# Softmax weights transposed on VectorE and through HBM instead of on TensorE, in a four-layer encoder

## What is computed

```python
logits = jnp.einsum('bqhmd,bkhmd->bmhqk', qb, k).astype(jnp.float32) + bias
probs = jax.nn.softmax(logits, axis=-1)
w = (probs[:, 0] - lam * probs[:, 1]).astype(v.dtype)
return jnp.einsum('bhqk,bkhe->bqhe', w, v)
...
logits = jnp.einsum('bshd,bmhd->bhsm', q, km).astype(jnp.float32)
probs = jax.nn.softmax(logits, axis=-1).astype(vm.dtype)
return jnp.einsum('bhsm,bmhd->bshd', probs, vm).reshape(b, s, XATTN_W)
```

## Time and profile before

| | |
|---|---|
| median of 3 runs | 1246.14 us (1246.03 to 1246.64) |
| span of the profiled execution | 1244.7 us |
| TensorE busy | 1235.2 us, 99%, 7370 instructions |
| VectorE busy | 1024.4 us, 82% |
| ScalarE busy | 730.3 us, 59% |
| DMA engines, mean busy share of the weight queue | 55.5%, 229.27 MB moved |

### The profile page before, as it was taken

How to read it: one execution, slowest core, us unless ns; L and a number is a source line. 1 busy time by engine, 2 the same in 40 slices (tenths; PEclk the granted TensorE clock), 3 DMA queues, 4 the chain that set the end, 5 groups by cost and what they waited for, 6 DMA issues and landing times.

```text
span 1244.7 us, 19689 instructions
## 1 busy us (share of the span) xinstructions
PE 1235.2 (99%) x7370; PEld 1082.9 (87%) x7370; DVE 1024.4 (82%) x1599; ACT 730.3 (59%) x1190; POOL 20.1 (2%) x29
## 2 busy tenths in 40 slices
PE   9999999999999999999999999999999999999997
PEld 7988888888999988888889888888888888888886
DVE  5876888889779888988887978988888776988887
ACT  6675765555766546555555546655554774755552
POOL 0001000000000100000000000000000001000000
PEclk9999999999999999999999999999999999999999
DMA  9834576554553345655655764656554533666651
GB/s 333 285 120 136 190 248 190 186 192 163 175 182 119 122 150 169 227 187 195 201 173 168 233 204 162 227 195 199 190 186 169 187 119 119 218 207 201 196 190 54
DMA packets 64539, 229.27 MB, mean 184 GB/s; under 512 B 7575, under 2 KB 9239, under 8 KB 63421
## 3 DMA queue, kind: packets, MB, share of 16 engines
q1 hardware_dynamic: 64444, 228.02, 55.5%
HBM read 226.93 MB, written 1.06 MB: 183 GB/s over the span
## 4 chain that ended last, share of the span: by engine, by line
PE 97%; DMA 1%; SPq 1%; DVE 0%; issue 0%; ACT 0%; DVEq 0%
PE pair L768 28%; PE acc L862 21%; PE pair L771 14%; PE pair L800 4%; PE pair L801 4%; PE pair L802 4%; PE acc L768 2%; PE acc L843 2%; PE acc L842 2%; PE acc L841 2%; PE pair L1022 2%; DMA raw<-in_stream 1%; PE pair L825 1%; PE pair L827 1%; PE pair L829 1%; PE acc L931 1%
## 5 line engine op out<-in xcount | busy, mean ns | idle before, releaser
L1278 DVE TENSOR_TENSOR w_lo<-raw,w_hi 128x1024 fp32r<-128x1024 f32 x400 | 482.6, 1221 | 105.3 <-ACT w_hi L1040 103.7
L1040 ACT ACTIVATE w_hi<-raw 128x1024 fp32r<-128x1024 f32 x400 | 420.5, 1058 | 213.2 <-PE pair L771 70.8
L768 PE MATMUL pair<-xT,w_hi 128*128 128x512 f32 x1520 | 477.8, 396 | 0.0
L771 PEld LDWEIGHTS pair<-xT,w_lo 128*128 128x128 f32 x1520 | 285.5, 188 | 67.2
L771 PE MATMUL pair<-xT,w_lo 128*128 128x256 f32 x1520 | 298.6, 278 | 0.0
L768 PEld LDWEIGHTS pair<-xT,w_hi 128*128 128x128 f32 x1520 | 233.8, 189 | 3.2 <-issue 0.3
L1087 ACT ACTIVATE hid<-pair 128x512 f32<-128x512 f32 x88 | 52.6, 597 | 124.9 <-PE pair L771 124.9
L1319 DVE TENSOR_TENSOR hid<-pair,hid 128x512 f32<-128x512 f32 x88 | 60.7, 690 | 47.9 <-ACT hid L1087 47.7
L800 PE MATMUL pair<-xT,w_hi 128*128 128x256 f32 x336 | 97.8, 291 | 0.0
L801 PE MATMUL pair<-xT,w_hi 128*128 128x256 f32 x336 | 95.0, 283 | 0.0
L802 PE MATMUL pair<-xT,w_lo 128*128 128x256 f32 x336 | 94.9, 283 | 0.0
(11 more groups left out here) (223 smaller groups left out, 1661.9 us busy)
## 6 DMA issues: line engine op xcount, KB each, us to landing
raw<-in_stream SPq DMA_DIRECT2D x400, 512.0 KB, 4.6
gains<-in_ln SPq DMA_DIRECT2D x8, 1024.0 KB, 8.4
bias<-bias_scratch SPq DMA_DIRECT2D x2, 1152.0 KB, 9.0
raw<-in_stream SPq DMA_DIRECT2D x8, 256.0 KB, 6.6
x_tok<-in_x_t SPq DMA_DIRECT2D x4, 256.0 KB, 6.2
y_tok<-in_mem_t SPq DMA_DIRECT2D x2, 512.0 KB, 7.1
x_tok<-in_x SPq DMA_DIRECT2D x1, 1024.0 KB, 6.5
out<-x_tok SPq DMA_DIRECT2D x4, 256.0 KB, 2.0
```

The lines of the kernel that those rows point to most:

```text
L768: pe.matmul(bank, w_hi[:, slot, kk * P:(kk + 1) * P], xT[:, kk].rearrange("p a s -> p (a s)"), start=(kk == 0), stop=(kk == KT - 1), skip_ ...
L771: last = pe.matmul(bank[:, 0:SEQ], w_lo[:, slot, kk * P:(kk + 1) * P], xT[:, kk, 0, :], start=False, stop=(kk == KT - 1), skip_group_check ...
L1040: nc.scalar.activation(w_hi[:, u % SPLIT, :], raw[:, u % RAW, :], ACT.Copy).then_inc(hi_ready, 1)
L1278: v.tensor_tensor(w_lo[:, u % SPLIT, :], raw[:, u % RAW, :], w_hi[:, u % SPLIT, :].bitcast(F32), ALU.subtract).then_inc(lo_ready, 1)
```

## The change

TensorE no longer transposes the softmax weights. VectorE transposes them in 32x32 blocks ("xswap", "swap"): each block is turned in itself and stays in its band of 32 partitions. Four DMAs from SyncE's queue (one for each band) store the result to a scratch tensor in HBM, in rows of 256 floats (cross-attention) or 128 floats (heads), and one DMA ("xfetch", "fetch") reads it back so that the blocks stand in their transposed places. The scratch of each matrix is its own. The cross-attention's fetch lands where "xpv" reads it, in blocks (strided), and the heads' one is copied to `probT` by ScalarE ("spread"). In layer 1 the product "xprob" moves from VectorE to ScalarE. SyncE now walks the list of items as well, with the loads of weights in their places (`next_unit`), and the store of a swap waits for VectorE, the fetch for the four stores. In layers 0 and 3, "pv" of heads 4 and 5, "ms", "tok" and "scale" of the last pairs come one or more halves later.

```diff
-            at = {0: [it("xlog", 0), it("xlog", 1)], 1: [it("xexp", 0)], 2: [it("xexp", 1), it("xprob", 0)],
-                  3: [it("xprob", 1)], 5: [it("log", 0), it("log", 1)],
-                  6: [it("exp", 0), it("xturn", 0)], 7: [it("exp", 1), it("xpv", 0)],
-                  8: [it("prob", 0), it("xturn", 1)], 9: [it("prob", 1), it("xpv", 1), it("log", 2), it("log", 3), it("turnw", 0)],
-                  10: [it("exp", 2)], 11: [it("turnw", 1), it("exp", 3), it("prob", 2)],
-                  12: [it("prob", 3)], 13: [it("turnw", 2), it("log", 4), it("log", 5), it("pv", 0), it("pv", 1)],
-                  14: [it("ms", 0), it("exp", 4)], 15: [it("turnw", 3), it("tok", 0), it("exp", 5), it("prob", 4)],
-                  16: [it("scale", 0), it("prob", 5)], 18: [it("turnw", 4), it("pv", 2), it("pv", 3), it("turnw", 5)],
-                  19: [it("pv", 4), it("pv", 5), it("ms", 1), it("tok", 1), it("ms", 2)], 20: [it("scale", 1), it("tok", 2)],
-                  21: [it("scale", 2)]}
+            at = {0: [it("xlog", 0), it("xlog", 1)], 1: [it("xexp", 0)], 2: [it("xexp", 1), it("xprob", 0), it("xswap", 0)],
+                  3: [it("xprob", 1), it("xswap", 1), it("xfetch", 0)], 4: [it("xfetch", 1)],
+                  5: [it("log", 0), it("log", 1)], 6: [it("exp", 0)], 7: [it("exp", 1), it("xpv", 0)],
+                  8: [it("prob", 0), it("swap", 0)],
+                  9: [it("prob", 1), it("swap", 1), it("xpv", 1), it("log", 2), it("log", 3), it("fetch", 0)],
+                  10: [it("exp", 2), it("fetch", 1)], 11: [it("exp", 3), it("prob", 2), it("swap", 2)],
+                  12: [it("prob", 3), it("swap", 3), it("fetch", 2)],
+                  13: [it("log", 4), it("log", 5), it("pv", 0), it("pv", 1), it("fetch", 3)],
+                  14: [it("ms", 0), it("exp", 4)], 15: [it("tok", 0), it("exp", 5), it("prob", 4), it("swap", 4)],
+                  16: [it("scale", 0), it("prob", 5), it("swap", 5), it("fetch", 4)], 17: [it("fetch", 5)],
+                  18: [it("pv", 2), it("pv", 3)], 19: [it("ms", 1), it("tok", 1)],
+                  20: [it("scale", 1), it("pv", 4), it("pv", 5)], 21: [it("ms", 2), it("tok", 2)],
+                  22: [it("scale", 2)]}
+            for h, n in ((11, 0), (12, 1), (14, 2), (15, 3), (18, 4), (19, 5)):
+                at[h].append(it("spread", n))
...
-            at = {0: [it("xlog", 0), it("xexp", 0), it("xlog", 1), it("xexp", 1)], 1: [it("xprob", 0), it("xprob", 1)],
-                  4: [it("xturn", 0)], 5: [it("xpv", 0)], 8: [it("xturn", 1)], 9: [it("xpv", 1)]}
+            at = {0: [it("xlog", 0), it("xexp", 0), it("xlog", 1), it("xexp", 1)],
+                  1: [it("xprob", 0), it("xswap", 0), it("xprob", 1), it("xswap", 1)],
+                  2: [it("xfetch", 0)], 3: [it("xfetch", 1)], 5: [it("xpv", 0)], 9: [it("xpv", 1)]}
...
+                  2: [it("xswap", 0), it("xswap", 1)], 3: [it("xfetch", 0), it("xfetch", 1)],
+                  5: [it("xpv", 0)], 7: [it("xpv", 1)]}
...
+        swap_scratch = [nc.dram_tensor(f"swap_scratch{n}", [4, 4, 32, 256 if items[pos][0] == "xprob" else 128], F32, kind="Internal").ap()
+                        for n, pos in enumerate(prob_pos)]
...
+        def swap_source(n):
+
+            s = n % 2
+            return (ex[:, s] if items[prob_pos[n]][0] == "xprob" else prob[:, s, 1:2]).rearrange("p i t s -> p (i t s)")
+
+        def swap_target(n):
+
+            name, layer, h = items[prob_pos[n]]
+            if name == "prob":
+                return prob[:, n % 2, 0].rearrange("p t (a e) -> p (t a) e", a=2)
+            return (xprobT[:] if h else prob[:, 0].rearrange("p i t s -> p (i t s)")).rearrange("p (a e) -> p a e", a=4)
...
-            for u in range(RAW, 2 * nchunks):
+            def next_unit(u):
+
+                if u >= 2 * nchunks:
+                    return
...
+            for item in items:
+                name = item[0]
+                if name == "begin" and item[1] % 2:
+                    next_unit(item[1] // 2 * 2 + item[2] + RAW)
+                elif name == "lo":
+                    next_unit(item[1] + RAW)
+                elif name in ("xswap", "swap"):
+                    n = weights_of(item)
+                    sp.wait_ge(swapped, n + 1)
+                    for a in range(4):
+                        rows = slice(32 * a, 32 * a + 32)
+                        sp.dma_start(swap_scratch[n][a].rearrange("b i e -> i b e"), swap_source(n)[rows].rearrange(
+                            "i (b e) -> i b e", b=4)).then_inc(swap_stored[n % 2], 16)
+                elif name in ("xfetch", "fetch"):
+                    n = weights_of(item)
+                    if n >= 2:
+                        sp.wait_ge(swap_landed[n % 2], 16 * (n // 2))
+                    if name == "xfetch" and item[2] and item[1]:
+                        sp.wait_ge(xpv_done, 2 * item[1])
+                    sp.wait_ge(swap_stored[n % 2], 64 * (n // 2 + 1))
+                    sp.dma_start(swap_target(n), swap_scratch[n].rearrange("a b i e -> (b i) a e")).then_inc(swap_landed[n % 2], 16)
...
-                elif name == "xturn":
-
-                    n = prob_ord[pos]
-                    if ordinal[pos] == 0:
-                        pe.wait_ge(ident_landed, 16)
-                    pe.wait_ge(xprob_ready, ordinal[pos] + 1)
-                    for i in range(2):
-                        bank = side(pos, i)
-                        for k in range(2):
-                            for t in range(TT):
-                                last = pe.transpose(bank[:, k * SEQ + t * P:k * SEQ + (t + 1) * P],
-                                                    prob[:, n % 2, i, t, k * P:(k + 1) * P], ident[:])
-                        last.then_inc(xprob_turned, 1)
-                elif name == "turnw":
-                    n = prob_ord[pos]
-                    pe.wait_ge(prob_ready, ordinal[pos] + 1)
-                    bank = side(pos)
-                    for k in range(2):
-                        for t in range(TT):
-                            last = pe.transpose(bank[:, k * SEQ + t * P:k * SEQ + (t + 1) * P],
-                                                prob[:, n % 2, 0, t, k * P:(k + 1) * P], ident[:])
-                    last.then_inc(prob_turned, 1)
                 elif name == "xpv":
...
-                    pe.wait_ge(xprobT_ready, 2 * u + 2)
+                    n = weights_of(item)
+                    pe.wait_ge(swap_landed[n % 2], 16 * (n // 2 + 1))
                     pe.wait_ge(vm_ready, layer + 1)
                     bank = side(pos)
+                    weights = swap_target(n).rearrange("p a (i t k j) -> p i k t a j", i=2, t=2, k=2)
                     for k in range(2):
                         for i in range(2):
-                            last = pe.matmul(bank[64 * i:64 * i + 64, 0:SEQ],
+                            last = pe.matmul(bank[64 * i:64 * i + 64, 0:SEQ].rearrange("p (t a j) -> p t a j", t=2, a=4),
                                              vm[:, k, (2 * pr + i) * XHD:(2 * pr + i + 1) * XHD],
-                                             xprobT[:, i, k, :], start=(k == 0), stop=(k == 1))
+                                             weights[:, i, k], start=(k == 0), stop=(k == 1))
...
-                            last = pe.matmul(bank[:, at:at + P], probT[:, h, k, t * P:(t + 1) * P],
+                            last = pe.matmul(bank[:, at:at + P], probT[:, h, t, k, :],
...
-                        act.wait_ge(xprob_ready, logit_name[:n - 1].count("xlog"))
+                        act.wait_ge(swap_stored[n % 2], 64 * (n // 2))
...
+                elif name == "xprob" and layer_kind(item[1]) == "hgrn":
+                    n = weights_of(("xswap",) + item[1:])
+                    act.wait_ge(inv_ready, item[2] + 1)
                     for i in range(2):
-                        act.wait_ge(xprob_turned, 2 * u + i + 1)
-                        if u >= 1:
-                            act.wait_ge(xpv_done, u)
-                        nc.scalar.activation(xprobT[:, i], side_bank(pos, i)[:].rearrange(
-                            "p (k s) -> p k s", k=2), ACT.Copy).then_inc(xprobT_ready, 1)
-                elif name == "turnw":
-                    h, u = item[2], ordinal[pos]
-                    act.wait_ge(prob_turned, u + 1)
-                    nc.scalar.activation(probT[:, h], side_bank(pos)[:].rearrange(
-                        "p (k s) -> p k s", k=2), ACT.Copy).then_inc(probT_ready, 1)
...
+                    if n == 1:
+                        m = prob_ord["x", item[1], p // 2]
+                        act.wait_ge(swap_stored[m % 2], 64 * (m // 2 + 1))
...
-                        q = prob_pos[n - 2]
-                        if items[q][0] == "xturn":
-                            dve.wait_ge(xprob_turned, 2 * ordinal[q] + 2)
-                        else:
-                            dve.wait_ge(prob_turned, ordinal[q] + 1)
```

(58 more changed lines are left out.)

29 lines of the change are left out of this document (15 added, 14 removed).

## The result

The changed kernel takes 1275.76 us (median of 4 runs, 1274.65 to 1277.14) against 1246.2: ratio 1.0239, 95% interval 1.0224 to 1.0253, 29.6 us slower. The forecast was 1267.6 with a range of 1253 to 1284. The span of its profiled execution is 1272.8 us, 28.1 more than before. It was the fastest of the four executions (1274.65), so the profile accounts for 28.1 of the 29.6 us.

What follows compares the result with a forecast made beforehand. TensorE, without slack, was taken to bound the kernel. Net of saved transposes, layers 0 and 3 add 12.0 us, layer 1 3.7, layer 2 5.8: +21.5 on 1246.1 gives 1267.6 us, range 1253 to 1284.

Steps and rivals of the forecast that it cites:

- the main case: Whole kernel: TensorE waits for late softmax weights, +21.5 us over the transposes saved, 1267.6 us; chance 0.55.
- the waits cool TensorE: Rival: waits of 5 to 8 us drop TensorE's clock to 1.2 GHz; +6 to +11, 1274 to 1279; chance 0.2.
- What goes, 12.5 us: TensorE's removed transposes, eight xturn and twelve turnw: 4.5 us saved in layers 0 and 3, 1.74 in 1 and 2.
- The block transpose: On VectorE: upper bounds taken, 1.22 us for 1024 elements and 0.69 for 512, 18 us in all.
- Layer 2, fetch 0: First cross-attention fetch of layer 2: issued 695.9, landed 700.9; TensorE waits 7.6 us before xpv 0, net +5.8.
- Layer 1, fetch 0: First cross-attention fetch of layer 1: issued 343.6, landed 349.0; TensorE waits 5.4 us before xpv 0, net +3.7.
- Layers 0 and 3, checkpoints: Attention layers: delays at scale 0 (+1.0), scale 1 (+2.2) and the closing chunk; net +6.0 a layer, early waits swallowed.
- The late place of pv 4 and 5: Layers 0 and 3, behind scale 1: 7.9 us from pv 5's end to mixT_lo's uncovered, closing chunk at 118.6.
- Weight loads at no cost: SyncE's queue: late weight loads cost nothing, since five buffers cover them; without that cover 1 to 2 us each.
- TensorE busy about 1222: Expected sign in the profile after the change: TensorE's busy time about 1222.
- Landings: Fetches of swapped weights: 3.5 us at least, 4.6 median, 9.4 at most; under 3 or over 7 would show it wrong.
- hidden round trip: Rival: all fetches land before TensorE arrives, leaving 1246.1 - 12.5 = 1233.6 us; chance of clearly faster 0.07.

Runs made afterwards that it cites:

- number 6: Changed kernel with the first fetch of layers 1 and 2 issued right behind swap 1's stores, ahead of the weight load: 1271.8 us, ratio 1.0204.
- number 1: Changed kernel with idle 512-column matmuls on TensorE ahead of xpv 0, 28 in layer 1 and 38 in layer 2: 1277.0 us, ratio 1.0249.
- number 4: Kernel before, all TensorE transposes kept, with only the late end of the heads (pv 4 and 5 behind scale 1) in layers 0 and 3: 1252.03 us.
- number 2: Changed kernel with xpv 0 and 1 moved to half chunks 8 and 9 in layer 1, 9 and 11 in layer 2: 1266.32 us, ratio 1.0172.
- number 10: number 8 with xpv 1 moved from half chunk 14 to 15 in layer 2 and from 7 to 8 in layer 1: 1244.16 us, ratio 0.9986.
- number 8: Only the cross-attention's weights go by VectorE and scratch, spread out; heads by TensorE as in the kernel before: 1247.73 us, ratio 1.0017.
- number 5: Changed kernel with idle matmuls ahead of xpv 0 (13, 28, 38, 7 in layers 0 to 3) and scale 0 to 2 in layers 0 and 3: 1271.16 us.

## Why the prediction was right, and where it was off

The direction and the place of the main stalls were right; the time came out 8 us above the forecast, inside its range. What turned out is the main case together with the rival "the waits cool TensorE", which I had given 0.2 and whose 1274 to 1279 holds the measured 1275.8. By layers the forecast lacks 6.5 us (21.5 against 28.0): the waits before xpv 0 of layers 1 and 2 are 3.7 longer, the clock adds 4.2 there, and layers 0 and 3 come out 1.6 shorter than forecast, which hides a part. The rest, some 1.5 us, is what the profiled execution was below the medians. The upper end of the range was made of later fetches and a margin, not of the clock, so that the range held is in part luck.

- **What goes, 12.5 us:** right as far as the trace shows it. The step from one product to the next is 0.8 to 0.9 us shorter wherever an xturn stood, and in layer 3 the one from xpv 1 to pv 0, with three turnw in it, 1.3 (17.84 to 16.56) where the sum has 1.5.
- **The block transpose:** its line gives 1.245 us for 1024 elements and 0.712 for 512, where the upper bounds taken were 1.22 and 0.69. Those bounds were not bounds but nearly the value.
- **Layer 2, fetch 0:** swap 0 done at 704.87, forecast 691.2 + 13.5 of delay brought in = 704.7. TensorE arrives at 706.5, forecast 706.7. The fetch is issued at 710.01, forecast 709.4, and landed at 716.3, forecast 714.4. TensorE waits 9.6 us, forecast 7.6. So the mis-sized term is the landing: 6.3 us against 4.6 + 0.4. I took the median of the weight loads, but these are the median over all moments of the kernel, and the one in front of this fetch cost 2.4 (number 6).
- **Layer 1, fetch 0:** block transposes start at 344.10 and 345.70, forecast 338.4 and 340.1 with the 5.6 of layer 0 on top: right to 0.1. The stores end at 349.35, forecast 348.8, the fetch is issued at 349.95, forecast 349.2, and takes 6.4 us to its use instead of 5.4. TensorE waits 7.1 us, forecast 5.4.
- **The clock:** the term that the sum left out, and one of the signs of being wrong that the prediction names (a granted clock of 0.5 after a wait). It lengthens layers 1 and 2 by 2.5 and 1.7 us; by the runs with all waits filled it costs about 4.6. The rival priced a fall at 2.8 us, from the first matmuls of the kernel, which it set beside others in full flow. That reading was wrong: these matmuls multiply `zeros`, and two more of the same kind, right behind them, show what they take later:

```profile
5.09 0.64 PE L876 MATMUL acc<-zeros 128*128 128x256 f32 x2
```

These two of 256 columns take 0.53 us (the next work starts at 5.62), so four of 512 would take 2.1 at that pace. From 1.51 to 5.09 they took 3.6: a loss of 1.5 us, not 2.8, and at a granted clock that the page shows as full. That 2.8 lies near the 2.5 of layer 1 is luck. "TensorE: Matmul & The Clock Gate", "What's actually happening", of the Trainium skill says that an idle engine goes to half rate; here the trace agrees (0.50 granted during the waits of 7 and 10 us). A wait of 3.4 us did it in one execution (number 1, before scale 1 of layer 0) and not in another (the changed kernel, before xpv 0 of layer 0).

- **Layers 0 and 3, checkpoints:** scale 0 forecast 91.4, measured 91.22; scale 1 forecast 108.5, measured 107.52; closing chunk forecast 118.6, measured 118.16; fetch 2, which spread 2 waits for, landed at 86.9 in the forecast and at 86.6 in the trace. The step that was off is the early one: xpv 0 of layer 0 waits 3.4 us and not 1, since its fetch stands behind the stores of swap 1 and takes 6.4 us. It was swallowed later, as forecast. Layer 3 was to be the same as layer 0, +6.0, and is +4.8.
- **The late place of pv 4 and 5:** the sum had it as the 7.9 us that nothing covers, with TensorE waiting before the closing chunk for `mixT_lo`. That wait is 0.3 us; the real one, 1.7 us, stands before scale 2 for `a_out`. In the kernel before the late place costs 3.0 a layer (number 4), not 3.9.
- **Weight loads at no cost:** right. ScalarE's copies waited for raw 9.6 us against 8.0 before, and TensorE for none of them.
- **TensorE busy about 1222:** 1231.2, of which 6.3 are the lower clock; the rest, 3, is open.
- **Landings:** a fetch under 3 or over 7 us was another sign of being wrong. The twenty fetches took 2.7 to 8.4 us, so both ends were passed; TensorE waited for none of those over 7.
- **The rival "hidden round trip" (1233.6):** in layers 1 and 2 a use three to four half chunks later hides the trip, but 1233.6 also needs that VectorE and ScalarE have room for what they take over. They had none there: the waits of 3.6 and 3.4 us in number 2. I had costed the 18 us on VectorE as mattering "only where somebody waits" and never named who would wait once the fetch does not.

What stays open: why the fetch of layer 1 takes 5.8 us with no load ahead of it, which waits of some 2 to 4 us lower the clock, and why the heads' part stayed at 12 to 13 us when the cross-attention's part was spread.

## What to carry over

Transposes on a saturated TensorE cost only their own length, here 12.5 us. A way round them through VectorE, stores and a fetch took 12 to 13 us from the start of the block transpose to the use (344.10 to 356.33, 703.62 to 716.31), and costs nothing only where the use can stand that much later and the other engines have room for their share at that moment. Even so placed, the trips of number 10 gave back 2.0 of the 7.0 us of transposes they replace. Price a wait of the bounding engine as the wait plus half of what it does while the clock stays low after it, unless a later wait takes that up, as in layer 3 here.

## What the hardware showed

- Two long waits of TensorE (7.1 and 9.6 us) took its granted clock to 0.50, 2.2 and 3.1 us after the wait began; short ones, of 1.8 to 3.7 us, did so in some places and not in others. The run times of such kernels scatter: 1273.5 to 1280.0 in number 1, against 1251.9 to 1252.7 for number 4, whose waits stay under 2 us. The clock is a part of that: in number 8 the fastest run (1245.7) had a mean granted clock of 0.998 and the slowest (1253.7) 0.995, some 4 of the 8 us (an estimate, 0.003 x 1246). The four runs of number 5, all at 0.998 or 0.999, still lie 2.4 us apart.
- A fall of the clock costs time only where no later wait takes it up: nothing behind scale 0 of layer 3 in the changed kernel, but 2.1 and 1.4 us behind scale 1 in number 1.
- A block transpose of fp32 on VectorE takes what a product over as many elements takes (1.245 against 1.225 us for 1024), so it is no cheaper for VectorE than a second pass over the weights.
- A fetch of 512 KB for which TensorE waited was in use 3.8 to 7.0 us after its issue over all runs; what stood ahead of it in the queue made 2.4 us of that in one case (number 6, layer 2). The 64 and 128 KB stores landed in 2.2 and 2.4 us (medians).
